# The state-space kernel matrix built from 32-column pieces, shifted copies sent by DMA, and the skip term folded in

## What is computed

```python
dt = jnp.exp(log_dt)[:, None]
mag = jnp.exp(ar * dt)
ab_re, ab_im = mag * jnp.cos(ai * dt), mag * jnp.sin(ai * dt)
...                                   # c_re, c_im: zero-order hold
bb_re = c_re[..., None] * br - c_im[..., None] * bi
bb_im = c_re[..., None] * bi + c_im[..., None] * br
...                                   # x_t = ab * x_(t-1) + bb u_t, scanned over 1024 steps
y = (einsum('blgp,gcp->blgc', xr, C_re) - einsum('blgp,gcp->blgc', xi, C_im)
     + D_skip.reshape(SSM_GROUPS, SSM_GROUP) * uf)
y = gelu(y); a, g = split(y @ w_glu); return a * sigmoid(g)
```

## Time and profile before

| | us |
|---|---|
| three runs | 1471.65, 1471.96, 1472.15 |
| their median | 1471.96 |
| span of the profiled execution, first to last instruction | 1470.3 |
| TensorE busy in it | 1453.1 (99%) |
| VectorE busy | 1077.3 (73%) |
| ScalarE busy | 537.9 (37%) |
| POOL busy | 198.8 (14%) |

### The profile page before, as it was taken

One profiled execution on the slowest core, in us unless ns is written; L12 is line 12 of the kernel. 1 busy time (PEld: TensorE's weight loads), 2 busy tenths in 40 slices (PEclk: granted clock), 3 DMA queues, 4 the chain that ended last, 5 costly groups with the idle time before them and its releaser, 6 DMA issues.

```text
span 1470.3 us, 18474 instructions
## 1 busy us (share of the span) xinstructions
PE 1453.1 (99%) x7110; PEld 1210.6 (82%) x7110; DVE 1077.3 (73%) x1754; ACT 537.9 (37%) x697; POOL 198.8 (14%) x299
## 2 busy tenths in 40 slices
PE   8999999999999999999999999999999999999997
PEld 7888888888888888888898888888888888888885
DVE  6778668658757735446756869697969697978878
ACT  4445853323132253221234432333334343434332
POOL 0000010140211112101100212302020201011110
PEclk9999999999999999999999999999999999999999
DMA  8301120242213246424433436937372736464545
GB/s 329 73 29 58 58 87 29 100 130 95 73 64 107 65 135 206 146 68 133 172 102 113 129 115 207 308 114 229 98 242 88 228 115 208 134 180 145 168 165 186
DMA packets 113890, 199.65 MB, mean 136 GB/s; under 512 B 15224, under 2 KB 57248, under 8 KB 113824
## 3 DMA queue, kind: packets, MB, share of 16 engines
q0 software_dynamic: 46256, 118.53, 25.6%
q1 hardware_dynamic: 67552, 80.23, 16.5%
q10 hardware_dynamic: 16, 0.00, 0.0%
HBM read 163.08 MB, written 35.65 MB: 135 GB/s over the span
## 4 chain that ended last, share of the span: by engine, by line
PE 92%; DVE 5%; DMA 1%; issue 1%; ACT 1%; DVEq 0%; SPq 0%; ACTq 0%
PE bank L2056 53%; PE bank L2465 17%; PE bank L2485 14%; PE bank L2066 3%; PE bank L2096 1%; PE bank L2158 1%; DMA raw<-in_w_down_dram 1%; DVE tok L2024 1%; PE bank L2321 1%; PE bank L2306 1%; PE bank L2326 1%; PE bank L2291 1%; PE bank L2208 1%; PE bank L2263 1%; DVE acc L2033 1%
## 5 line engine op out<-in xcount | busy, mean ns | idle before, releaser
L2056 PE MATMUL bank<-hThi,whi 128*128 128x512 f32 x736 | 289.4, 393 | 0.1
L2056 PE MATMUL bank<-hThi,wlo 128*128 128x512 f32 x736 | 286.6, 389 | 0.0
L2056 PE MATMUL bank<-hTlo,whi 128*128 128x512 f32 x736 | 286.5, 389 | 0.0
L2056 PEld LDWEIGHTS bank<-hThi,whi 128*128 128x128 f32 x736 | 138.1, 188 | 30.1 <-issue 1.1
L1125 ACT ACTIVATE whi<-raw 128x1024 fp32r<-128x1024 f32 x91 | 95.3, 1055 | 183.4 <-DVE raw L1860 97.8
L2056 PEld LDWEIGHTS bank<-hThi,wlo 128*128 128x128 f32 x736 | 138.1, 188 | 29.2
L2056 PEld LDWEIGHTS bank<-hTlo,whi 128*128 128x128 f32 x736 | 138.2, 188 | 27.9
L1850 DVE TENSOR_TENSOR wlo<-raw,whi 128x1024 fp32r<-128x1024 f32 x91 | 111.0, 1220 | 33.6 <-ACT whi L1125 33.6
L2465 PE MATMUL bank<-hThi,whi 128*128 128x512 f32 x336 | 130.8, 389 | 0.5 <-DMA hTlo<-h_scratch 0.5
L2485 PE MATMUL bank<-whi,yhi 128*128 128x512 f32 x336 | 130.8, 389 | 0.4 <-DVE acc L1883 0.4
L2465 PE MATMUL bank<-hThi,wlo 128*128 128x512 f32 x336 | 130.7, 389 | 0.0
(11 more groups left out here) (412 smaller groups left out, 2764.8 us busy)
## 6 DMA issues: line engine op xcount, KB each, us to landing
hThi<-h_scratch POOLq DMA_DIRECT2D x42, 512.0 KB, 5.3
hTlo<-h_scratch POOLq DMA_DIRECT2D x42, 512.0 KB, 6.5
raw<-in_w_in_dram SPq DMA_DIRECT2D x34, 512.0 KB, 4.7
raw<-in_w_up_dram SPq DMA_DIRECT2D x32, 512.0 KB, 4.2
raw<-in_w_down_dram SPq DMA_DIRECT2D x32, 512.0 KB, 4.5
gate_scratch<-scr POOLq DMA_DIRECT2D x48, 256.0 KB, 2.3
tok<-gate_scratch POOLq DMA_DIRECT2D x24, 512.0 KB, 3.6
yhi<-h_scratch POOLq DMA_DIRECT2D x14, 512.0 KB, 5.8
```

What stands on the lines that cost most here:

```text
L2056: ins = T.matmul(dst, lhs(k)[p], rhs(k)[q], start=start and k == 0 and i == 0, stop=stop and k == kt - 1 and i == 2)
```

## The change

- TensorE: the `s5m` products take 32 columns of `Xp` (its last two 16-column blocks) as the stationary operand in place of 128 columns of `near`. Pair `pr` writes 32 partitions, `32 pr` to `32 pr + 31`, and 128 columns of its group's bank. There are still 16 products a round, of 64 rows, with the real ones first.
- VectorE copies the two banks to a new tile `kst`, as a copy of columns 16 to 127 and a product-add on columns 0 to 15, which adds D times the 16 x 16 identity (`id16`, `skip`). That is four instructions a round in place of the eight L1647.
- SP sends 32 DMAs a round from `kst` into `Mt`: for each pair `pr` and each step `j`, 16 partitions x 2 groups x (128 - 16 j) elements, in `kernel_matrix`. It is called after the loads of gates 5, 7, 9 and 11. In it SP waits for the `s5m` banks to be taken and for the `s5y` banks of the round before. TensorE waits for all of them (`k_loaded`) ahead of both parts of `s5y`, and VectorE, before it writes `kst` again.
- The skip term goes into `Mt`. `Dbc`, `near`, `s5_du` and POOL's three instructions a round are gone. D is loaded by 16 DMAs of 16 partitions x 2 single elements into `skip`, on `s5_in`, whose waits rise from 112 to 352. POOL issues them before `gates_out(2)`.
- The `s5y` banks are taken by ScalarE (two copies, after its work for gate `4+2r`) and no longer by VectorE.

```diff
@@ -188,7 +188,8 @@
         sinkx = sb("sinkx", [P, 16, 4])
         ldt = sb("ldt", [NPAIR, 2])
         rho = sb("rho", [P, NPAIR])
-        parity = sb("pad", [P, 40])[:, 0:2]
+        pad = sb("pad", [P, 40])
+        id16, skip = pad[:, 0:SG], pad[:, SG:SG + 8]
         raw = sb("raw", [P, 2, UNIT])
         whi = sb("whi", [P, 2, UNIT], f32r)
         wlo = sb("wlo", [P, 2, UNIT], f32r)
@@ -242,9 +243,9 @@
             sB = ov("sB", [P, 2, NPAIR, SG])
             Bb = ov("Bb", [P, 2, NPAIR, SG])
             cpk = ov("cpk", [P, 2, NPAIR, SG])
-            Dbc = ov("Dbc", [P, W512])
+            kst = ov("kst", [P, 2, P])
+            free_k = ov("free_k", [P, 1280])
             Xp = ov("Xp", [P, 2, RP, P])
-            near = ov("near", [P, 2, RP, P])
             ca = ov("ca", [P, 2, RP, 9 * SG])
             Mt = ov("Mt", [P, 2 * RP, P])
             wT = ov("wT", [P, 2, RP, P])
@@ -318,10 +319,10 @@
         y_loaded = [sem(f"y_loaded{s}") for s in range(4)]
         y_hi, y_lo = sem("y_hi"), sem("y_lo")
         s5_in, s5_small_in = sem("s5_in"), sem("s5_small_in")
-        s5_near, s5_dt = sem("s5_near"), sem("s5_dt")
-        s5_parity, s5_even = sem("s5_parity"), sem("s5_even")
+        s5_dt, skip_zero = sem("s5_dt"), sem("skip_zero")
+        k_loaded = sem("k_loaded")
         s5_trig, s5_trig_done = sem("s5_trig"), sem("s5_trig_done")
-        s5_x, s5_ca, s5_xs, s5_du, gelu_done = sem("s5_x"), sem("s5_ca"), sem("s5_xs"), sem("s5_du"), sem("gelu_done")
+        s5_x, s5_ca, s5_xs, gelu_done = sem("s5_x"), sem("s5_ca"), sem("s5_xs"), sem("gelu_done")
         acc_zero = sem("acc_zero")
         merged = sem("merged")
         m_hi, m_lo = sem("m_hi"), sem("m_lo")
@@ -525,8 +526,22 @@
             gate(0)
             for s in range(2):
                 load(U_U + s, cols(U_U + s, w_in[512 * s:512 * s + 512, C_U:C_U + W512], BT))
+            def kernel_matrix(r):
+
+                for g in range(2):
+                    wait_taken(sp, FIRST[f"s5m{r}"] + g)
+                if r:
+                    for e in range(2):
+                        wait_full(sp, FIRST[f"s5y{r - 1}"] + e)
+                for pr in range(RP):
+                    for j in range(STEP):
+                        sp.dma_start(Mt[SG * j:SG * j + SG, 2 * pr:2 * pr + 2, SG * j:P],
+                                     kst[32 * pr + SG:32 * pr + 2 * SG, :, 0:P - SG * j]).then_inc(k_loaded, 16)
+
             for i in range(1, 12):
                 gate(i)
+                if i > 3 and i % 2:
+                    kernel_matrix((i - 5) // 2)
             for s in range(2):
                 u = U_MERGE_A + s
                 v = raw[:, u % 2, :].rearrange("p (k c) -> p k c", k=BT)
@@ -593,6 +608,7 @@
             g.affine_select(out=ident[:, :], in_=ident[:, :], compare_op=ALU.not_equal, fill=1.0, base=0,
                             pattern=[[-1, P]], channel_multiplier=1).then_inc(consts, 1)
             g.memset(ones, 1.0).then_inc(consts, 1)
+            g.memset(pad[:, :], 0.0).then_inc(skip_zero, 1)
             x = a["x"][0].rearrange("(c i) d -> i c d", i=STEP)
             pool.wait_ge(tile_in[7], 16)
             for k, name in enumerate(("ssm_A_re", "ssm_A_im")):
@@ -630,21 +646,14 @@
             for k, name in enumerate(("ssm_C_re", "ssm_C_im")):
                 for d in range(2):
                     g.dma_start(craw[:, k, :, d, :], a[name][0].rearrange("(r g) o p -> (g o) r p", r=4)).then_inc(s5_in, 16)
-            g.dma_start(Dbc[:, :], a["ssm_D"][0].partition_broadcast(P)).then_inc(s5_in, 16)
+            pool.wait_ge(skip_zero, 1)
+            skip_in = a["ssm_D"][0].rearrange("(r q g c) -> q c r g", r=4, q=RP, g=2)
+            for pr in range(RP):
+                for r in range(4):
+                    g.dma_start(skip[32 * pr + SG:32 * pr + 2 * SG, 2 * r:2 * r + 2], skip_in[pr, :, r, :],
+                                allow_slow_non_contiguous=True).then_inc(s5_in, 16)
             gates_out(2)
-            pool.wait_ge(s5_in, 112)
             for r in range(4):
-                for e in range(2):
-                    wait_taken(pool, FIRST[f"s5a{r}"] + e)
-                sl = uc[:, 8 * r:8 * r + 8, :, :]
-                dd = Dbc[:, P * r:P * r + P].rearrange("p (g c) -> p g c", c=SG).unsqueeze(2).to_broadcast([P, 8, STEP, SG])
-                g.tensor_tensor(sl, sl, dd, mul).then_inc(s5_du, 1)
-
-                pool.wait_ge(s5_x, r + 1)
-                for ri in range(2):
-                    dst = near[:, ri, :, :].rearrange("p a (i c) -> p a i c", c=SG)
-                    src = Xp[:, ri, :, 7 * SG:8 * SG].unsqueeze(2).to_broadcast([P, RP, STEP, SG])
-                    g.tensor_copy(dst, src).then_inc(s5_near, 1)
                 gates_out(3 + 2 * r)
                 gates_out(4 + 2 * r)
 
@@ -966,18 +975,11 @@
                 for ri in range(2):
                     copy_out(n0 + 2 + ri, wT[:, ri, :, :].rearrange("p g c -> p (g c)"))
                 gates(3 + 2 * r)
+                gates(4 + 2 * r)
                 for e in range(2):
-                    n = FIRST[f"s5m{r}"] + e
-                    wait_full(act, n)
-                    if r == 0:
-                        act.wait_ge(s5_parity, 1)
-                    for m in range(4):
-                        rows = slice(32 * m, 32 * m + 32)
-                        src = banks[n % 8][rows, :].rearrange("p (b x) -> p b x", b=4)[:, :, 0:P - 32 * m]
-                        dst = Mt[rows, :, :].rearrange("p (q g) x -> p g q x", g=2)[:, e, :, 32 * m:P]
-                        ins = A.activation(dst, src, ACT.Copy, scale=parity[rows, 0:1])
-                    ins.then_inc(s5_even, 1)
-                gates(4 + 2 * r)
+                    n = FIRST[f"s5y{r}"] + e
+                    copy_out(n, uc[:, 8 * r:8 * r + 8, :, :].rearrange("p (q g) i o -> p g q (i o)", g=2)[:, e],
+                             banks[n % 8][:, :].rearrange("p (q x) -> p q x", q=4))
 
             def y_piece(pc, hi):
 
@@ -1555,15 +1557,12 @@
                 V.tensor_copy(yst2[:, q % 2, :].rearrange("p (i s t) -> p s i t", i=4, s=2),
                               banks[n % 8][:, :].rearrange("p (s i t) -> p s i t", s=2, i=4)).then_inc(bank_free[n % 8], 1)
 
-            blocks = ident[:, :].rearrange("p (m j c) -> p j m c", j=2, c=SG)
-            for j in range(2):
-                do(V.reduce_sum(t1[:, 4 * j:4 * j + 4], blocks[:, j], AX.X))
-                do(V.reduce_sum(parity[:, j:j + 1], t1[:, 4 * j:4 * j + 4], AX.X))
-            dve.sem_inc(s5_parity, 1)
+            dve.wait_ge(skip_zero, 1)
+            do(V.reduce_sum(id16, ident[:, :].rearrange("p (m c) -> p c m", c=SG), AX.X))
             do(V.memset(Mt[:, :, :], 0.0))
             do(V.memset(xs[:, :, :, 0:1], 0.0))
             prep_lo(dve, U_GATE[2] + 1)
-            dve.wait_ge(s5_in, 112)
+            dve.wait_ge(s5_in, 352)
             temps = (t1, t2, t3, t4)
             cmul([Bb[:, ri, :, :] for ri in range(2)], [sm[7 + ri].unsqueeze(2).to_broadcast([P, NPAIR, SG]) for ri in range(2)],
                  [sB[:, ri, :, :] for ri in range(2)], [tt[:, 0:256].rearrange("p (a b) -> p a b", b=SG) for tt in temps])
@@ -1572,8 +1571,6 @@
             def make_x(r):
 
                 pr = slice(RP * r, RP * r + RP)
-                if r:
-                    dve.wait_ge(s5_near, 2 * r)
                 cmul([Xp[:, ri, :, 0:P].rearrange("p a (b c) -> p a b c", b=8) for ri in range(2)],
                      [pwR[:, ri, pr, :].unsqueeze(3).to_broadcast([P, RP, 8, SG]) for ri in range(2)],
                      [Bb[:, ri, pr, :].unsqueeze(2).to_broadcast([P, RP, 8, SG]) for ri in range(2)], t512)
@@ -1637,25 +1634,17 @@
                      [z5[:, ri, :, 0:c127] for ri in range(2)],
                      [tt[:, 0:RP * c127].rearrange("p (a b) -> p a b", a=RP) for tt in temps])
                 dve.sem_inc(s5_xs, 1)
-                for e in range(2):
-                    n = FIRST[f"s5m{r}"] + e
-                    dve.wait_ge(s5_even, 2 * r + e + 1)
-                    for m in range(4):
-                        rows = slice(32 * m, 32 * m + 32)
-                        odd = banks[n % 8][rows, :].rearrange("p (b x) -> p b x", b=4)[:, :, 0:P - 32 * m - SG]
-                        dst = Mt[rows, :, :].rearrange("p (q g) x -> p g q x", g=2)[:, e, :, 32 * m + SG:P]
-                        ins = V.scalar_tensor_tensor(out=dst, in0=odd, scalar=parity[rows, 1:2], in1=dst, op0=mul, op1=add)
-                    ins.then_inc(bank_free[n % 8], 1)
+                if r:
+                    dve.wait_ge(k_loaded, 16 * RP * STEP * r)
+                for g in range(2):
+                    n = FIRST[f"s5m{r}"] + g
+                    wait_full(dve, n)
+                    V.tensor_copy(kst[:, g, SG:P], banks[n % 8][:, SG:P])
+                    V.scalar_tensor_tensor(out=kst[:, g, 0:SG], in0=id16, scalar=skip[:, 2 * r + g:2 * r + g + 1],
```

(20 more changed lines are left out.)

## The result

| | before | changed |
|---|---|---|
| median of 4 runs, us | 1471.81 | 1477.93 |
| lowest to highest | 1470.63 to 1472.15 | 1477.38 to 1479.92 |
| span of the profiled execution | 1470.3 | 1475.6 |
| TensorE busy | 1453.1 | 1449.4 |

The ratio is 1.0046, with a 95% interval of 1.0034 to 1.0058: 6.1 us slower, where 3.5 was forecast, and inside the forecast range of 1469 to 1486. TensorE's work fell by 3.7 us and its waits grew by more.

What follows compares the result with a forecast made beforehand. TensorE, busy 99% of the span, was taken as the bound. Terms -3.0 (s5m) + 5.2 (Xp) + 1.3 (clock) + 0 (copies) = +3.5 us, giving 1475.5 against 1471.96, range 1469 to 1486.

Steps and rivals of the forecast that it cites:

- SP's issues: 32 copies into Mt a round, issued by SP: 0.40 us each, 4.2 us to spare before s5y, cost 0.
- the break-even of 0.53: Issue cost in us per copy on SP in round 0 above which TensorE would wait for Mt before s5y.
- The late copies: Rival: SP's issues cost more than 0.53 us, TensorE waits before s5y; at 0.63, 7.4 us, time 1482.9; chance 0.18.
- The clock: After TensorE's idle time of about 4 us before the Xp transposes, clock drops to 1.2 GHz: 1.3 us, bounds 0 and 2.6.
- the wait for Xp: TensorE in round 0 waits for VectorE's Xp, ready at 328.9 instead of 323.7: 5.2 us lost, once.
- The start of round 0: 16 small D loads on POOL fill s5_in at 322.8 (0.50 an issue, 4.6 landing): 5.2 us lost, ends 2.9 and 9.4.
- The sinks' 6.8 us: Issue-to-landing time of sinkb's single-element DMAs, used for the D loads' upper end, a loss of 9.4 us.
- s5m: TensorE's state products overlap further on smaller tiles: gain 0.75 us a round, 3.0 in all, range 0 to 6.0.
- The limit of 25 ns between starts: TensorE product starts never closer than about 25 ns; by that the s5m gain would be 1.2 us a round.
- ScalarE's two copies of s5y: Two copies of 0.6 us after the fourth gate eviction, 1.7 us or more before TensorE needs the banks; worth 0.
- The late gate loads: SP's loads of gates 6, 8 and 10 are held behind the copies; the first moves from 341 to 366, hidden.
- The attention weights: Last load on SP moves from 501 to about 527, wanted at 537: hidden; at 0.63 an issue, landing about when wanted.

Runs made afterwards that it cites:

- the probe: Changed kernel plus 24 extra DMAs on SP in its idle time before round 0, four of each of six shapes, into unused space; one execution, 1480.16 us.

## Why the forecast had the side right and the size too small

**SP's issues: the step that failed.** I took 0.40 us and a cost of 0, for two reasons: issues of 0.33 to 0.40 were "the more usual", and the slow ones moved 512 KB. It measured 0.59 with 0.04 between and one slow issue a round, 0.68 on average. That is above the break-even of 0.53 which the prediction gave. Both reasons fail.

The first fails on the trace of before. SP's weight loads come in pairs, and the second of a pair, issued directly behind the first, is the slower. The rows of all these loads, of one pair, and of the first of that pair alone:

```profile
L488 SPq DMA_DIRECT2D raw<-in_w_in_dram x42: 367/508/5226, 20.6 to 470.8; - x42
L488 SPq DMA_DIRECT2D raw<-in_w_in_dram x2: 368/438/508, 341.1 to 341.5; - x2
L488 SPq DMA_DIRECT2D raw<-in_w_in_dram x1: 368/368/368, 341.1 to 341.1; - x1
```

Of SP's 158 issues before, 86 stand directly behind another, with a median of 0.51 us; the 72 behind a pause have 0.37. In a fan of 32, all but the first stand behind another. 0.51 with 0.04 between is 0.55, above the break-even already. The second reason fails by the probe: neither size nor partitions set the price of these copies; both sides on the chip do, and no row of the trace of before had that.

The late copies were a rival, at 7.4 us in all; its waits measured 6.8. So the mechanism and the place stood in the text, with a chance of 0.18. That the price agrees is partly luck. In round 0 the issues were slower than that rival's 0.63, but SP started 0.8 us earlier (351.96, against 352.8), TensorE came 1.3 us later (at 373.0, against 371.7), and landing took 1.8 us in place of 2.3.

**The clock.** I put it behind the wait for Xp, where it stayed at 1.00. It fell behind the first wait for copies, a wait that I had costed at 0: 1.6 us in the profiled execution.

**The start of round 0.** POOL's issues were right (0.507 against 0.50; 16 in 8.01 us). The landing was not: 1.8 us for the last, not 4.6, and below the 2.3 that I had as the lower end. POOL also came to these loads 0.8 us earlier than before (309.91, against 310.73). `s5_in` was full at 319.2, not at 322.8, and TensorE lost 2.1 us, not 5.2. The sinks' 6.8 us, the row nearest in kind (single elements), was the worst guide. The rule that single elements become one descriptor each, from the Trainium skill, "DMA: Bandwidth & Descriptors", Rules for kernel authors, gave no visible price here: 32 single elements per DMA landed in 1.8 to 5.1 us.

**s5m.** I took the middle, 0.75 a round. The upper end, 1.49, was nearly right: 1.37. The starts come in four groups of eight, 0.11 to 0.13 us from group to group, where one product of 128 x 128 took 0.124. The trace agrees with the rule of the Trainium skill in "TensorEngine Tiling (Array Packing)", Key Properties, that tiles work independently. The limit of 25 ns between starts, of the Trainium skill in "TensorE: Matmul & The Clock Gate", section "Wait — 56ns, not 53.3ns?", doesn't hold here. The 32 products span 0.67 us, and one of them lasts 0.27, so the starts lie within 0.40 us, 13 ns apart on average.

**What hid.** ScalarE's two copies of s5y and VectorE's four instructions (0.74 us from first to last, I took 1.0) cost nothing. The late gate loads didn't either. The attention weights, which I had landing "at about the time" they are wanted for slow issues, did just that: ScalarE waited 2.3 us and TensorE not at all.

The errors of the terms were -3.1 (Xp), -1.3 + 1.6 (clock), -2.5 (s5m) and +6.8 (copies), +1.5 together. The profiled execution went from 1470.3 to 1475.6, 5.3 us for a forecast of 3.5, and the medians differ by 6.1. That the forecast came so near is luck: errors of -6.9 us and +8.4 us cancelled. It had slower for the start of round 0 and the clock behind it, 6.5 us; those gave 2.1. What made the kernel slower was the copies and the clock behind them, 8.4 us, which it had at 0.

## What to carry to other kernels

Count a fan of small DMAs by the issue time on its queue first, and take that price from a DMA with the same kinds of source and target that stands directly behind another: here 32 copies of 2 to 16 KB cost 21 us of one queue, and half of them on another queue cost no wait. Put a wait directly ahead of the first instruction that needs it: 2.0 us of products that stood behind the wait for no reason were worth 8 us here. A fan of small loads ahead of a semaphore that starts a stage belongs where its queue is idle; of this change, with these edits, 5 us of gain are left (ratio 0.9962).

## What the runs showed of the hardware that I had not expected

- A DMA with both sides on the chip takes SP 0.59 to 0.62 us to issue, whatever its partitions (16, 64, 128) and dimensions; one from HBM of the same size takes 0.42. On POOL a copy of the same kind takes 0.50 (16 in 7.97 us).
- Products of 64 rows x 32 columns overlap nearly eightfold in float32 (0.60 us for 32 to the next product, against 1.99 with two side by side; 0.67 to the end of the last), with the real and imaginary part of one tile directly behind each other too (0.71).
- Of SP's weight loads in the trace of before, the second of a pair took 0.51 us to issue and the first 0.37.
- About one in 32 of the copies' issues on SP took 0.9 to 1.8 us, and each of these overlapped a packet of a queue that the profile calls "instruction" (37 of 37, against 72 of 1115 others). Whether that is the cause isn't tested.
- TensorE's granted clock fell to its lower level after waits of 1.81, 2.02, 2.23, 2.25 and 2.36 us in five places of four executions, and stayed at 1.00 after waits of 2.34 and 2.48. Where it fell behind the first wait of the changed kernel, it cost 1.6 us.
